# Spread values of the chunked mixers in four buffers, and memory projections in groups of four

## What is computed

```
z = x @ w_in                         # split among four head groups
A: mLSTM, chunkwise                  # 4 heads of 64, state C, n, m
     C_new = carry_w * C + einsum('bjh,bjhk,bjhv->bhkv', w_j, kc, vc)
B: retention, chunkwise, rotary      # 4 heads of 64, state R
     R_new = g_chunk * R + einsum('jh,bjhk,bjhv->bhkv', zeta, kc, vc)
C: RG-LRU after a convolution        D: RWKV-7 time mixing
x = LN(alpha * x + concat(A, B, C, D) @ w_out)
kp = mem_prompt @ xa_wk;  vp = mem_prompt @ xa_wv    # also outputs
x = LN(alpha * x + cross_attention(x, kp, vp or the caches))
x = LN(alpha * x + relu(x @ w_up)**2 @ w_down)
```

## Time and profile before

| | us |
|---|---|
| median of 3 runs | 2424.02 |
| lowest, highest | 2422.4, 2424.86 |
| profiled execution | 2421.59 |
| its span, first to last instruction | 2419.6 |
| TensorE busy in it | 2349.6 (97%) |
| VectorE busy | 1010.7 (42%) |
| ScalarE busy | 456.0 (19%) |
| mean granted clock of TensorE | 0.979 |

### The profile page before, as it was taken

How to read it: one execution, slowest core, us unless ns; L and a number is a source line. 1 busy time by engine, 2 the same in 40 slices (tenths; PEclk the granted TensorE clock), 3 DMA queues, 4 the chain that set the end, 5 groups by cost and what they waited for, 6 DMA issues and landing times. The chain is left out here.

```text
span 2419.6 us, 31493 instructions
## 1 busy us (share of the span) xinstructions
PE 2349.6 (97%) x13278; PEld 1718.0 (71%) x13278; DVE 1010.7 (42%) x1851; ACT 456.0 (19%) x963; POOL 113.2 (5%) x208
## 2 busy tenths in 40 slices
PE   7999999999999999999999999999999999999997
PEld 6877775555874888888887777655468658888886
DVE  4252234644033644665132422446421345447742
ACT  2341222111131222100023321220112212220000
POOL 0011100100000000000001111000000000000000
PEclk9999998989999999999999999989899999999999
DMA  8111003145243211322232111133333331222320
GB/s 280 36 70 38 23 15 93 62 122 212 99 141 122 87 70 70 105 70 70 70 124 70 36 37 36 36 97 105 126 139 138 124 139 35 103 71 70 105 70 37
DMA packets 137675, 215.04 MB, mean 89 GB/s; under 512 B 35528, under 2 KB 69632, under 8 KB 137408
## 3 DMA queue, kind: packets, MB, share of 16 engines
q1 hardware_dynamic: 135232, 208.84, 25.4%
q10 hardware_dynamic: 2304, 4.20, 0.5%
HBM read 198.43 MB, written 14.58 MB: 88 GB/s over the span
## 5 line engine op out<-in xcount | busy, mean ns | idle before, releaser
L589 PE MATMUL psum<-xT,ring 128*128 128x256 f32 (+1 forms) x1536 | 357.4, 394 | 3.4 <-ACT xT L320 1.6
L589 PEld LDWEIGHTS psum<-xT,ring 128*128 128x128 f32 x1536 | 291.6, 191 | 64.6 <-issue 3.5
L636 PE MATMUL psum<-xT,ring 128*128 128x256 f32 (+1 forms) x768 | 223.6, 417 | 0.1
L2132 PE MATMUL psum<-tmp 128*128 128x272 f32 x768 | 181.4, 393 | 0.0
L2132 PEld LDWEIGHTS psum<-tmp 128*128 128x128 f32 x768 | 145.8, 190 | 30.8 <-issue 0.8
L636 PEld LDWEIGHTS psum<-xT,ring 128*128 128x128 f32 x768 | 133.8, 191 | 41.9 <-issue 15.2
L633 PE MATMUL psum<-ring,ext 128*128 128x512 f32 x256 | 119.2, 606 | 4.5 <-ACT ext L1662 4.5
L2233 PE MATMUL psum<-big,ring 128*128 128x256 f32 (+1 forms) x512 | 118.5, 393 | 0.1
L2543 PE MATMUL psum<-ring,big 128*128 128x512 f32 x256 | 113.1, 595 | 0.0
L736 PE MATMUL psum<-ring,big 128*128 128x512 f32 x256 | 111.9, 594 | 0.0
L2233 PEld LDWEIGHTS psum<-big,ring 128*128 128x128 f32 x512 | 97.0, 190 | 20.3 <-DMA ring<-in_w_down 0.7
(11 more groups left out here) (475 smaller groups left out, 3265.1 us busy)
## 6 DMA issues: line engine op xcount, KB each, us to landing
ring<-in_w_down SPq DMA_DIRECT2D x16, 2048.0 KB, 8.1
ring<-in_w_in SPq DMA_DIRECT2D x14, 2048.0 KB, 8.1
ring<-in_w_up SPq DMA_DIRECT2D x14, 2048.0 KB, 7.8
big<-in_cache_mem_k SPq DMA_DIRECT2D x16, 1024.0 KB, 5.0
ring<-in_xa_wk SPq DMA_DIRECT2D x4, 2048.0 KB, 7.8
ring<-in_xa_wv SPq DMA_DIRECT2D x4, 2048.0 KB, 10.6
ring<-in_w_out SPq DMA_DIRECT2D x4, 2048.0 KB, 10.0
tmp<-in_cache_mem_v SPq DMA_DIRECT2D x8, 1024.0 KB, 10.0
```

The lines of the kernel that those rows point to most:

```text
L589: ins = pe.matmul(ps[:m, :w], lhsT_list[k], rhs(k)[:, c], start=(k == 0), stop=(k == n - 1))
L636: ins = pe.matmul(bank[:, :c.stop - c.start], wring[:, n % 2, k, i * P:(i + 1) * P], xTv[:, k, c], start=(k == 0), stop=(k == KC - 1))
L2132: ins = pe.matmul(ps[:, :HT], left[:, k, :], right[:, k, :], start=(k == 0), stop=(k == KH - 1))
```

## The change

The spread values get four buffers for each mixer, one for each head: two where they were and two in `xtok`, which held mixer D's operands and state before. A new function `own_values` makes all four with no wait between them, after waiting for the transfers of mixer D's state out of `xtok` (`Sout`). In tile 4's round of VectorE's loop it is called for B ahead of `weights("B", 4)` and for A behind `weights("A", 4)`, so ahead of `normalise(3)`. TensorE waits for a pair's two values at once, and the semaphore by which VectorE learned that a buffer was read is gone. `FILL_AB` goes from (10, 10, 8) to (8, 8, 8) units: each group has four products.

```
-            FILL_AB = (10, 10, 8)
+            FILL_AB = (8, 8, 8)
```

```
                             for pr in range(2):
                                 ps = bk.begin(pe, (pre + "sts", pr), (2, 4)[pr] if pre == "A" else (1, 5)[pr])
+                                pe.wait_ge(sig[pre + "vx"], sig.at(pre + "vx", 2 * pr + 2))
                                 for a in range(2):
-                                    h = 2 * pr + a
-                                    pe.wait_ge(sig[pre + "vx"], sig.at(pre + "vx", h + 1))
                                     ins = pe.matmul(ps[a * HD:a * HD + HD, :], k_[:NS, pr, a * HD:a * HD + HD],
-                                                    x_[:NS, h % 2, :, :].rearrange("p a b -> p (a b)"), start=True, stop=True)
-                                    if a == 0:
-                                        sig.up(ins, pre + "vxread")
+                                                    x_[2 * pr + a][:NS].rearrange("p a b -> p (a b)"), start=True, stop=True)
```

```
+                    def own_values(pre):
+                        n, T = NS, 4
+                        v_, x_ = (vt_a[T % 2], vx_a) if pre == "A" else (vt_b, vx_b)
+                        own = const("own")[:n].unsqueeze(2).broadcast_to([n, NB, HD])
+                        bk.given(v, (pre + "tr", T))
+                        v.wait_ge(sig["Sout"], sig.at("Sout", 16 * (NB + 2)))
+                        for h in range(H):
+                            sig.up(tt(x_[h][:n], v_[:n, h // 2, (h % 2) * HD:(h % 2) * HD + HD].unsqueeze(1)
+                                      .broadcast_to([n, NB, HD]), own, ALU.mult), pre + "vx")
+
                     def decode_states(pre):
                         n, T = NS, 4
-                        v_, x_ = (vt_a[T % 2], vx2) if pre == "A" else (vt_b, vx2_b)
-                        own = const("own")[:n].unsqueeze(2).broadcast_to([n, NB, HD])
-                        bk.given(v, (pre + "tr", T))
-                        for h in range(H):
-                            if h == 2:
-                                v.wait_ge(sig[pre + "vxread"], sig.at(pre + "vxread", 1))
-                            if h == 3:
-                                bk.take(v, (pre + "sts", 0))
-                            sig.up(tt(x_[:n, h % 2], v_[:n, h // 2, (h % 2) * HD:(h % 2) * HD + HD].unsqueeze(1)
-                                      .broadcast_to([n, NB, HD]), own, ALU.mult), pre + "vx")
```

```
                         keys_values("B", T)
+                        if T == 4:
+                            own_values("B")
                         weights("B", T)
                         weights("A", T)
+                        if T == 4:
+                            own_values("A")
                         if T:
                             normalise(T - 1)
```

More of the change, by code:

```diff
@@ L508, in build @@
             qx = cols(tmp, dbase + 2736, 2, P)
-            vx2 = cols(big, 22 * NT + 1536, 2, NB, HD)
+            vx_a = [cols(big, 22 * NT + 1536, NB, HD), cols(big, 22 * NT + 2048, NB, HD), cols(xtok, 0, NB, HD), cols(xtok, 512, NB, HD)]
             qpad_b = cols(big, 22 * NT, 2, 2, P)
@@ L514, in build @@
             qspad_b = cols(big, 22 * NT + 2560, 2, 2, NS)
-            vx2_b = cols(big, 16 * NT, 2, NB, HD)
+            vx_b = [cols(big, 16 * NT, NB, HD), cols(big, 16 * NT + 512, NB, HD), cols(xtok, 1024, NB, HD), cols(xtok, 1536, NB, HD)]
             Rs = cols(big, 28 * NT, 2, NB, HD)
@@ L1112, in outputs @@
                         w_, k_, v_ = (Wm_a[T % 2], kw_a[T % 2], vt_a[T % 2]) if pre == "A" else (Wm_b, kw_b, vt_b)
-                        q_, x_ = (qspad, vx2) if pre == "A" else (qspad_b, vx2_b)
+                        q_, x_ = (qspad, vx_a) if pre == "A" else (qspad_b, vx_b)
                         if T == 4:
```

## The result

The changed kernel takes 2402.14 us (six runs, 2399.69 to 2405.05) against 2424.78 beside it: ratio 0.9908, with a 95% interval of 0.9895 to 0.9921. The forecast was 2413.1 with a range from 2404 to 2420.5, so the gain was taken at half its size: 10.9 forecast, 22.6 measured. Three more measurements of the same code, on other occasions, gave gains of 17.8, 17.9 and 18.9 us; the first was the largest, but all four lie well beyond the forecast of 10.9. The times of these three, 2405.1 to 2405.4 us, lie 1.1 to 1.4 us inside the range, and the first lies 1.9 us outside it.

What follows compares the result with a forecast made beforehand. TensorE bounds the kernel, 97% busy: its work, few waits and clock. Per layer -2.25 - 0.33 - 2.3 + 2.3 - 2.85 = -5.4 us, -10.9 for both, so 2413.1 us from 2424.0; range 2404 to 2420.5.

Steps and rivals of the forecast that it cites:

- Groups of four: Chunk loop: with four products per group, three waits a layer for ScalarE's bank copy go, 4.5 us over both layers.
- The cover of the (T, 1) groups: Chunk loop: products covering VectorE thin from five to four, 0.92 us; costed at nothing, at most 4 us a layer.
- Spread values: State products at the loop's end: making the values earlier removes their waits, 0.33 us (retention) and 2.3 (mLSTM) a layer.
- the next late step: mLSTM end: VectorE's divisions, state additions and normaliser delay the transpose at L1203, so 2.3 us gained, not 2.42.
- VectorE's slack: Before normalise(3): the moved values fit VectorE's idle time, leaving 1.3 us before TensorE needs bank 1.
- The slower case: Moved values take 1.8 us each instead of 0.64, making VectorE late: 2429 us, 3%.
- The tenth group: Four products between the last two tiles: 2.3 us more at the low clock, 2.85 saved in the mLSTM part, per layer.
- the first case: End of loop: clock falls before the four products and returns within them, 6.0 us for them; the forecast, 2413.1 us, 60%.
- the second 13%: End of loop: clock falls only after the four products, -8.8 us a layer, 2406.5 us; rival, 13%.
- Clock B: End of loop: clock does not fall at all, -12.9 us a layer, 2398.3 us; rival, 7%.
- w_out and the stores: After the loop: w_out's half slab, asked for about 6 us later, lands in time; nobody waits for the state stores.
- the clock's cases: End of loop: alternatives for when the clock falls and rises, from 2398.3 us (no fall) to 2421.6 (late rise, 12%).

## Why the prediction was wrong

- **Groups of four: right.** 4.5 us forecast, 5.6 measured for both layers. The starts in the earlier trace rows had said more than the idle times: the interrupted group occupies 426.70 to 432.0, 5.3 us for five products, where five in a row take 4.4. The cover of the (T, 1) groups held, and no wait appeared in the loop.
- **Spread values: the term that failed.** I summed the idle times of L1169, 5.5 us, capped them by the next late step and took 0.33 + 2.3 a layer, 5.3 in all; the runs gave 11.2 and 11.9, both layers together. The step that failed is "TensorE runs two pairs of state products of 2.47 us each": I took 2.47 as the work of a pair. It is 1.74 of work and up to 0.7 of waiting that the list does not show, because the second head's value arrives while the first head's matmul still runs. The kernel before with aligned halves (late values) against the changed kernel with the group ahead of the loop (early values), both with the clock low, shows the whole of it; the DVE line of each is the last step of the normaliser that reads PSUM:

```profile
506.08 2.48 PE L1169 MATMUL psum<-big,tmp 32*64 32x512 f32 x4 [2.10 <-DVE big L1569]
508.88 2.47 PE L1169 MATMUL psum<-big,tmp 32*64 32x512 f32 x4 [0.32 <-DVE big L1569]
...
512.75 0.40 PE L1203 MATMUL psum<-con,tmp 128*36 128x128 f32 x1 [0.46 <-DVE sm L1588]
...
512.40 0.17 DVE L1586 TENSOR_TENSOR tmp<-tmp,psum 128x16 f32<-128x16 f32 x1 [0.17 <-PE psum L1177]
```

```profile
504.63 1.98 PE L1168 MATMUL psum<-big,tmp 32*64 32x512 f32 x4
506.37 1.95 PE L1168 MATMUL psum<-xtok,tmp 32*64 32x512 f32 x4
...
509.72 0.40 PE L1200 MATMUL psum<-con,tmp 128*36 128x128 f32 x1 [0.46 <-DVE sm L1585]
...
509.37 0.17 DVE L1583 TENSOR_TENSOR tmp<-tmp,psum 128x16 f32<-128x16 f32 x1 [0.17 <-PE psum L1174]
```

  From L1126 (498.57 and 499.44) to the transpose it is 14.2 and 10.3 us: 3.9 saved, 2.42 of listed waits and 1.5 that stand in no line, where I had 2.3. It is 3.9 in the second layer too. The cap was wrong at this clock: the wait for the normaliser is 0.46 us in both, and in both VectorE itself waits 0.17 us for TensorE's product in between, so VectorE was not late. At the high clock it is late, as I had said of this step: TensorE waits 0.76 to 2.21 us for it in ten ends of the changed kernel. Retention's part gave 7.1 against 6.3 us in the first layer, though its clock fell earlier with early values, and 8.1 against 6.4 in the second. That makes 10.3 of the 11.2.
- **VectorE's slack: right.** The last value ends at 485.23 and normalise(3) starts there; bank 1 was free in time and no wait stands before the first L1168. The slower case did not come about.
- **The tenth group: its parts right, its sum not resolved.** -0.55 a layer forecast, -0.7 to -1.1 by the medians, which can't be told from nothing. The group takes 5.1 to 6.2 us where the clock falls ahead of it (5.6 to 6.4 forecast) and 3.7 where it falls behind, and the mLSTM's 64 matmuls take 2.03 in every profile of the changed kernel. Whether the clock falls ahead of the group and comes back inside it, or falls behind it, moves an end from 19.8 to 16.5 us (3.35 forecast). I had given the first case 60% and the second 13%; of the ten ends in five profiles (one of them of the kernel with a wait for each head) seven took 19.8, one 18.1 (the fall inside the group) and two 16.5 us. The reading behind it was weak: I took the fall to come 3.7 us after the 64 matmuls begin, from the first layer, but in the second layer of the same profile it came 2.7 us after (1687.9, from 1685.15). And the group starts 4.3 and 5.8 us after them, not 6.5, since the pairs are shorter.
- **Clock B: not seen.** In none of these ten ends did the clock stay high to the head means.
- **w_out and the stores: right.** The half slab landed in time and L736 never waited.
- **The range.** Its low end came from the clock's cases. Every one of them carried the same mis-sized term, so they moved together, and the low end of 2404 was too high by what all of them lacked, about 6 us.
- **Still open.** The first measurement gave 3.7 to 4.8 us more than the three later ones. Its interval overlaps with theirs, and no run shows a cause; that the time fell outside the range by 1.9 us owes something to this. The gain of the later ones, 18.9 in the last, goes beyond the forecast by the values' 6 us and small differences in the other terms.

## What to carry to other kernels

A list of idle times can be far below what late operands cost where two instructions overlap on the engine (5.3 us here, for 11.2 to 11.9): take start-to-start times and compare them with the same form at the same clock when its operands are there. Before a merged row is used as a price of work, look at its records one by one: a gap of about the producer's pitch between two starts points to a wait, whatever the busy time says. And give each term of a sum its own uncertainty; a range over rival mechanisms does not cover a term that all of them share.

## What the runs showed of the hardware

Two matmuls of 32 rows and 64 columns that write different halves of a bank's partitions overlap. At the low clock a record of each lasts 1.08 us, they start within 0.05 us of each other, and from a pair of four records to the next pair it is 1.70 to 1.74 us; at the high clock it is 0.89. A late value stretches such a pair from 1.74 to some 2.4 us without any idle time in the profile.

The Trainium skill (TensorE: Matmul & The Clock Gate, "Part 1: The HAM clock gate") says that the clock follows how busy TensorE has been. The row above with TensorE busy 13.85 of 14.00 us at a clock of 0.50 does not agree, if busy means having an instruction in flight: the stretch holds mostly matmuls of four columns and of 32 rows. The clock came back only under the head means, at 515.2 us, as before the change (520.5).
